# Gathered expert rows in four chains of three cells instead of five, with all eight mixing units of the weights kept on chip

## What is computed

```python
merged = (sigmoid(g_a) * (a_out @ w_proj_a) + sigmoid(g_b) * (b_out @ w_proj_b))
x = x + merged @ w_out
# peer: per token 8 heads, 16 experts each, out of 16384
q = (xc @ w_q).reshape(PEER_BLOCK, PEER_HEADS, 2, PEER_DK)
s = einsum('chsk,hsnk->chsn', q, sub_keys)          # two lists of 128 scores
...                                                  # top 16 of each, top 16 of their sums
u = u_tab[eidx]
act = gelu(einsum('chkd,cd->chk', u, xc))
out = einsum('chk,chkd->cd', g * act, v_tab[eidx])
```

## Time and profile before

| | us |
|---|---|
| median of 3 runs | 3051.58 (3050.4 to 3053.53) |
| the profiled execution | 3053.22, of which its span is 3051.4 |
| PE / DVE / ACT / POOL busy in the span | 2442.7 / 2162.8 / 1207.0 / 1121.5 |
| DMA moved | 1215.48 MB, 398 GB/s over the span |

### The profile page before, as it was taken

The page is one execution under the profiler, slowest core; times in us unless marked ns, Lnnn a source line. Parts: engine busy times, 40 slices in busy tenths (PEclk is TensorE's granted clock), DMA queues, the critical chain, the costliest instruction groups (busy, mean ns, idle before and its releaser), DMA issues.

```text
span 3051.4 us, 43432 instructions
## 1 busy us (share of the span) xinstructions
PE 2442.7 (80%) x14628; PEld 1180.5 (39%) x14628; DVE 2162.8 (71%) x5374; ACT 1207.0 (40%) x3786; POOL 1121.5 (37%) x1048
## 2 busy tenths in 40 slices
PE   9997768899887778899877768888977776766776
PEld 7863324565343324455233324455433321111111
DVE  7757887776479876676468987676558897554445
ACT  2224444433345444333335444433244444333333
POOL 0023443433334443333333443333334444433332
PEclk9998888999988879999988879999988886677667
DMA  4569999999999999999999999999999999999998
GB/s 156 200 242 408 407 411 421 420 417 414 412 420 412 421 420 420 421 404 421 420 421 406 406 419 413 421 419 420 419 414 419 409 416 419 419 421 421 420 421 344
DMA packets 176079, 1215.48 MB, mean 398 GB/s; under 512 B 22360, under 2 KB 22744, under 8 KB 31472
## 3 DMA queue, kind: packets, MB, share of 16 engines
q0 software_dynamic: 148608, 1082.20, 85.9%
q1 hardware_dynamic: 25744, 126.19, 10.4%
q10 hardware_dynamic: 1504, 4.33, 0.4%
HBM read 1208.12 MB, written 4.51 MB: 397 GB/s over the span
## 4 chain that ended last, share of the span: by engine, by line
DMA 29%; issue 22%; PE 20%; DVE 15%; POOL 11%; ACT 2%; DVEq 0%; ACTq 0%; POOLq 0%; SPq 0%
DMA arena<-in_uv,arena 15%; DMA arena<-in_vu,arena 14%; POOL arena L802 11%; PE psum L2277 7%; DVE arena L1824 6%; PE psum L2165 5%; PE psum L2321 3%; DVE arena L1306 3%; ACT arena L856 2%; DVE arena L1314 1%; DVE arena L1687 1%; PE psum L2341 1%; PE psum L2353 1%; DVE arena L1645 1%; DVE arena L1310 0%
## 5 line engine op out<-in xcount | busy, mean ns | idle before, releaser
L1824 DVE CUSTOM_DVE_ANT_0 arena<-arena 128x1024 f32<-128x1024 f32 x1024 | 1246.7, 1224 | 762.5 <-DMA arena<-in_uv,arena 392.4
L2277 PE MATMUL psum<-arena 64*64 64x512 f32 x8184 | 1282.6, 730 | 556.2 <-ACT arena L856 504.4
L856 ACT ACTIVATE arena<-arena 128x1 f32<-128x1 f32 (+3 forms) x3252 | 932.6, 289 | 1630.8 <-DVE arena L1824 1449.6
L802 POOL DMA_INDIRECT arena<-in_vu,arena x517 | 554.5, 1073 | 987.8 <-DVE arena L1824 690.7
L802 POOL DMA_INDIRECT arena<-in_uv,arena x515 | 563.8, 1095 | 920.6 <-DVE arena L1824 810.5
L2277 PEld LDWEIGHTS psum<-arena 64*64 64x64 f32 x8184 | 276.1, 150 | 1370.2 <-ACT arena L856 1102.9
L2165 PE MATMUL psum<-arena 128*128 128x256 f32 (+1 forms) x2656 | 653.7, 403 | 2.8 <-DVE arena L1314 1.7
L2165 PEld LDWEIGHTS psum<-arena 128*128 128x128 f32 x2656 | 519.3, 200 | 201.9 <-issue 122.7
L1306 DVE TENSOR_TENSOR arena<-arena 128x256 f32<-128x256 f32 (+11 forms) x562 | 249.9, 471 | 12.9 <-ACT psum L856 0.8
L856 ACT ACT_TABLE_LOAD x119 | 152.7, 1283 | 10.9 <-DVE arena L1306 7.0
L856 ACT ACTIVATE arena<-psum 128x256 f32<-128x256 f32 (+5 forms) x246 | 95.2, 400 | 108.9 <-PE psum L2165 79.6
(11 more groups left out here) (139 smaller groups left out, 1048.0 us busy)
## 6 DMA issues: line engine op xcount, KB each, us to landing
arena<-in_w_in SPq DMA_DIRECT2D x56, 1024.0 KB, 9.1
arena<-in_w_q SPq DMA_DIRECT2D x34, 1024.0 KB, 9.6
arena<-in_vu,arena POOLq DMA_INDIRECT x517, 11.3
arena<-in_uv,arena POOLq DMA_INDIRECT x515, 11.3
arena<-in_w_ab SPq DMA_DIRECT2D x11, 512.0 KB, 10.0
arena<-in_keys SPq DMA_DIRECT2D x17, 256.0 KB, 7.7
arena<-in_w_out SPq DMA_DIRECT2D x8, 512.0 KB, 16.0
arena<-in_x_tok SPq DMA_DIRECT2D x8, 512.0 KB
```

Of the source, the lines that this page charges most:

```text
L802: pool.indirect_dma_start(rows_[:, first:first + 2 * D], None, table, bass.IndirectOffsetOnAxis(column, 0)).then_inc(uv_in[at % UV], 16)
L856: return nc.scalar.activation(out, in_, f, **kw)
L1824: V.tensor_tensor_reduce(out=u, in0=u, in1=hn, scale=1.0, scalar=0.0, op0=ALU.mult, op1=ALU.add, accum_out=dots_[:, b % DOTS, k:k + 1]).th ...
L2277: ins = mm(PV[o:o + HP, half], dg[r:r + HP, PAIR * (b % 2) + k], cells[r:r + HP, v_cell(place(c, i)), at:at + 512], start=(i % (SLOT // 2) ...
```

## The change

`CHAINS` goes from 5 to 4, so there are 12 cells instead of 15 and a gather waits for the dot of the fourth gather before it, not the fifth, and for the values of the eighth, not the tenth. The three cells become homes of `w_ab` units 5 to 7, so all eight units are loaded once and stay; the parking and its waits are gone.

```diff
-CHAINS = 5
+CHAINS = 4
...
-RESIDENT = tuple(("w_out", m) for m in range(8)) + tuple(("w_ab", m) for m in range(5))
+RESIDENT = tuple(("w_out", m) for m in range(8)) + tuple(("w_ab", m) for m in range(8))
 GLU_W = tuple(("w_glu", m) for m in range(4))
-MIX_PARKED = tuple(("w_ab", m) for m in LAST_FIRST[0:3])
-MIX_CELLS = (13, 14, 12)
-HOMES = RESIDENT + GLU_W + MIX_PARKED
+HOMES = RESIDENT + GLU_W
...
         homes = [R.take(D) for _ in RESIDENT] \
-            + [rows_[:, GLU_AT + DB * k:GLU_AT + DB * k + DB] for k in range(QT)] \
-            + [cells[:, k] for k in MIX_CELLS]
+            + [rows_[:, GLU_AT + DB * k:GLU_AT + DB * k + DB] for k in range(QT)]
...
-                        if held & set(MIX_CELLS):
-                            pool.wait_ge(unit, U_MIX1 + 1 + max(k for k, cell in enumerate(MIX_CELLS) if cell in held))
```

More of the change, by code:

```diff
@@ L501, in build @@
         GLU_AT = 6 * D
-        assert W.at <= T.at + GLU_AT and min(MIX_CELLS) * D >= GLU_AT + QT * DB
+        assert W.at <= T.at + GLU_AT
         homes = [R.take(D) for _ in RESIDENT] \
-            + [rows_[:, GLU_AT + DB * k:GLU_AT + DB * k + DB] for k in range(QT)] \
-            + [cells[:, k] for k in MIX_CELLS]
+            + [rows_[:, GLU_AT + DB * k:GLU_AT + DB * k + DB] for k in range(QT)]
         dg = R.take(2 * PAIR, HP)
```

## The result

| | before | after |
|---|---|---|
| median, us | 3051.51 | 3131.63 (3124.7 to 3137.42) |
| ratio, 95% interval | | 1.0262 (1.0250 to 1.0274) |
| span of the profiled execution | 3051.4 | 3126.2 |

A forecast was written before the change was run, and what follows sets the result against it. DMA bytes were taken to bound the kernel while rows are in flight. Saving -5, dips +9 and holds +5 gave +9 us on 3053.22, about 3060.5 against the median; range 3044 to 3080.

The forecast's parts named there:

- The bound: Whole kernel: DMA bytes set the time while rows are in flight, a gather taking 2.49 us at 421 GB/s.
- the values: A gather's wait for the eighth row's matmul, not the tenth's: taken as 0, up to 5 us where PE is full.
- The saving: Six w_ab loads fewer in each of chunks 1 to 3: 5 us taken, bounds 0.4 to 11.2.
- the 0.2 us of slack: End of mixing, chunk 2: PE ends the needed unit 0.2 us before DVE's last step; 2.5 us saved in each of chunks 2, 3.
- F: A gather's time from issue to landing with nothing ahead: 6.6 us taken, leaving four chains 1.8 us of reserve.
- Rival A: Reserve is enough and the saved bytes count in full, lone gather near 5.3 us: 3040 to 3045 us, chance 0.12.
- The dips: List stages: landings too short for four chains, 0.3 us for each of 31 top-k heads, 9 us; bounds 0 to 37.
- The test: DMA stays full while time to landing exceeds a lone gather's; shortest landings less 2.49 us fell short by 0.1 to 1.2.
- Rival C: Reserve breaks, 16 engines not ending a row together; heads and many scan pieces run dry: 3078 to 3095 us, chance 0.10.
- The count: List stages: a dip comes at most once a head of top-k, 31 heads from the second of chunk 0 on.
- The place: List stages and chunk 1's mixing use the reserve; the quiet stretch was priced at 0.
- The two holds: At the start and the end of chunk 1's mixing, each costs up to one row: 5 us, bounds 0 and 5.

The follow-up runs named there:

- e1: Kernel before, all chains, cells and loads kept; a gather waits for the dot of the fourth gather before it, not the fifth: 3137.37 us against 3051.74.
- e2: Kernel before with five chains; a gather waits only for the values of the eighth gather before it, not the tenth: 3053.55 us, ratio 1.0006.
- e3: Kernel before with five chains; in chunks 1 to 3 w_ab units 5 to 7 are read from homes of units 0 to 2, not loaded again: 3043.59 us.
- e7: Kernel before; in chunk 3's quiet end, three groups of batches wait for the third, second and first dot before: 3292.16 us, one execution.
- e8: Kernel before; extra DVE multiplies in the quiet end as holds of 3.75 or 7.5 us, depth 4 in the second stretch, else 5: 3076.04 us.
- e10: Kernel before; short extra DVE multiplies (2.44 or 1.22 us) in the quiet end without added loads, at depths 5, 4, 4, 5: 3061.80 us.
- e6: Kernel before; only gathers of projections, scans, glu, mixing and w_out wait for the fourth dot before, the others for the fifth: 3092.64 us, ratio 1.0130.
- e5: Kernel before; only gathers issued while top-k lists are made wait for the fourth dot before, the others for the fifth: 3096.81 us against 3051.94.
- e9: Kernel before; 32 unused 1 MB weight loads in the quiet end, at depths 5, 4, 4, 5, the last two with DVE holds: 3133.06 us.

## Why the prediction was wrong, step by step

**What held.** The bound (bytes, as long as rows are in flight) and the place of the cost (a gather's wait for its dot) are right: e1 is the whole of it. So are the sign; the quiet end, 2.49 us a row with 8.4 to landing; the values at 0 (e2); and 1210.8 MB with six loads less. GB/s fell in the list windows, but by up to 6%, not by one at most. The dots' waits for data in 900 to 1000, 2.6 us in the earlier trace rows, are 10.7 now:

```profile
DVE arena L1819 <- DMA arena<-in_vu,arena: 6.4, 6, 2.8
DVE arena L1819 <- DMA arena<-in_uv,arena: 4.3, 6, 1.3
```

**The saving: right within the noise, its reason not borne out.** 5 us were taken. With five chains e3 measured 8.2. Chunk 1 gave nothing, as read from PE's unbroken chain. Chunks 2 and 3 gave about 4 each and not 2.5, so with five chains the stock of rows in the cells didn't cap it and the 0.2 us of slack in the earlier trace rows was no limit. With four chains, e1 less the change is 5.5 us (uncertain by 5 and 4 us), which cannot tell 5 from 8.

**F: 1 us too long, and not the cause.** 6.6 was taken, between 5.3 and 7.9, and a lone row takes 5.6 (e7). By rows, four chains thus keep 2.8 us, not 1.8. Rival A said that it would win with F under 5.7. F was, and A lost by 90 us. The error therefore isn't in that number but in what it was compared with. The formula of the Trainium skill (DMA: Bandwidth & Descriptors, "Anatomy of one DMA — SWDGE (gpsimd) path"), 4.4 us by estimate, is 1.2 us under the measured landing, and would have missed in the same direction.

**The dips, 9 us, where the missing row costs 86: the step that failed.** It had three parts.
- *The test.* "The DMA stays full as long as that is above F", with the shortest landing of a window as the sign. Depth 3 in e7 loses 0.5 us a row with 0.3 us in hand, and e8 loses 10% with no landing under 7.2. A landing shows when the last of 16 engines is through with a row. It says nothing of those that were through earlier and had nothing left, and in e8's second stretch fewer than 16 packets are in flight for 21% of the time. So a landing well above F proves nothing, and the earlier trace rows, less 2.49, were no bound. The Trainium skill (DMA: Bandwidth & Descriptors, "Queues, rings and completion order") says that each engine works off a ring of its own; e7's lone rows, whose 16 last packets lie 0.34 to 0.82 us apart, agree. Rival C had this mechanism, engines that don't end a row together, and the scan pieces too, but hung it on F of 7 or more and on the quiet stretch, and neither came; its 3078 to 3095 us are 37 short.
- *The count.* One dip a head, 31 of them. e8 and e10 show that each hold of DVE between two dots counts, 0.2 us for 1.22 us, 0.6 to 1.1 for 2.4 to 3.9, and a head has several. 42 us over 344 rows of list stages are 0.24 us for each batch of two.
- *The place.* The prediction named the list stages and chunk 1's mixing as the places that use the reserve, and left the projection and scan stages at 0. e6 puts 41 us there.

**The two holds, 5 us.** After is 11.3 us behind at dot 72, the first in lists, and e5 7.6. Neither hold was isolated; both lie within the stages above.

**The range.** The dips' bounds were 0 to 37 us, from 1.2 us a head, and the point was taken near the lower one since "few are as deep as the deepest". Even its upper end, with the holds and the values, gave only 3095. It left the scans out entirely.

**What stays open.** Single engines of the 16 stand still while others have bytes, and packets grow long; why they do so while every landing still takes 7.2 us or more (e8) is not shown, so no formula for the reserve comes out of this. And in e9 depth 4 stays full with one load for four gathers, while the scan stages, with one load of 1 MB for some seven gathers, lose 0.08 us a row. How the loss goes with the rate of loads wasn't measured, nor which of their pieces on DVE cost most.

**A better version.** No run that computes the whole layer beats before: to have e3's 8.2 us and five chains, the three units need 12 KB more in each partition, and no kernel here has found them.

## What to carry to other kernels

Before a stage of prefetch is taken away, change only the wait's depth, one constant, with all the buffers left in place: e1 gave the whole cost without any of the rewriting. A depth that is enough in a steady stretch says little of a stretch in which the consumer comes and goes, and the price is bent: 0, 86, 513 us for five, four and three rows. Don't take the time of one transfer for the reserve that a queue needs: rate is lost while rows are still queued. The sign is GB/s below the plateau while the busy share still reads near 1.00.

## What the runs showed of the hardware

- A gather of 1.05 MB alone: 5.6 us from issue to landing. Its first packet starts after 1.64 us and its last ends after 5.2 (e7); among others a gather takes 2.49 us at 421 GB/s.
- The DMA share isn't a measure of the rate: 1.00 with 405 GB/s, 0.98 with 378 and 383, 1.01 with 421. Packets that take longer count as busy.
- With four rows in flight and DVE held (e8), 3.2% of the engines' time has no packet and 6.8% goes into packets longer than the usual 309 to 324 ns.
- POOL's issue of a gather, 0.94 us, takes 1.68 to 1.97 beside two-input work on DVE. The Trainium skill (GPSIMD Engine Reference, "1. Specifications") names SBUF interfaces shared with VectorE, with contention for instructions with two SBUF inputs; the longer issues fit that, though no row shows the interface. It isn't what costs here: e10's fourth stretch has such issues and loses nothing.
- With one 1 MB load for four gathers, four rows in flight and DVE held in every batch, the engines keep 419 GB/s (e9); without loads, holds at depth 4 leave 378 to 405 (e8, e10).
